# Host layouts for cached keys and up weights, and chunk weights on ScalarE's queue, in a hybrid decoder layer

## The chip, the cores and the metric

One NeuronCore of a Trainium2 chip runs the whole layer in one launch. The metric is device time in microseconds (us). All data is float32. Arrays arrive in the chip's memory in the layout that the host gives them; work of the host is outside the measured time.

## The reference, cut to what matters

The layer has 2048 prompt rows and 8 sample sequences of 4 rows each. Every sample sequence has 8192 past positions in 64 pages of 128 keys and values, found through a page table. What is computed (norms, reshapes and the prompt's own attention left out):

```python
past_k = cache_k[page_table].reshape(8, 8192, 8, 64)      # 8 heads of 64 channels
past_v = cache_v[page_table].reshape(8, 8192, 8, 64)
z = einsum('bqhd,bkhd->bhqk', q, concat(past_k, k)) * 64 ** -0.5 + sb_bias
a = exp(log_sigmoid(z) + sum of log_sigmoid(-z) over all later keys)   # stick breaking
o_sb = einsum('bhqk,bkhd->bqhd', a, concat(past_v, v))
x = x + gate1 * (concat(o_sb, o_mlp) @ w_out)              # 1024 x 1024
h2 = rms_norm(x) * (1 + scale2) + shift2
up = h2 @ w_up                                             # 1024 x 5632
g, v = split(causal depthwise convolution, width 3, of up)
y = x + gate2 * ((silu(g) * v) @ w_down)                   # 2816 x 1024
```

## The kernel before

The program has four stages, each a block in which all engines start together after the last: `prepare` (modulation vectors and constants, span 0 to about 112 us), `project_in` and `attend_prompt` (to 1263), `attend_new_keys` (the samples' own new keys, to 1286) and `finish_layer` (the rest). This change touches the first and the last two.

**finish_layer** handles the prompt in NCH = 4 chunks of CT = 512 rows, with the same plan each, and then the 32 sample rows. A chunk is: the output projection (`tok` events of phase 0: four 1 MB weight loads), the norm and its transposes (`turn`), the up projection (22 tiles f of 2 x 128 columns; a tile is seven products `mul(f, p)` of four 128x128 by 128x256 matmuls each), and the down projection (`tok` events of phase 1: 16 loads of 768 or 256 KB). A matmul of float32 shows as two records of TensorE in the trace, so a product is eight. ScalarE copies four of the seven products out of PSUM (`collect`: L1571, L1574, L1579, L1582) and applies the last tap (L1592); VectorE adds the other three (L1721, L1727, L1731) and the other taps (L1758); GpSimd makes three sums of each up tile's blocks and changes one block in place (`weight_sums`, L1814 to L1819), then multiplies the gated rows.

**Weights** go through a ring `w` of RING = 3 slots. There are LOADS = 42 loads a chunk. All are issued by SP from one list, `load_order`: load n goes where the last use of n - 3 stands in the plan, after a wait for TensorE's counter that this use is over (`wait_used`, L1331). An up tile is two DMAs of 512 KB, whose rows in memory are 128 columns, 512 bytes, long.

**The samples' past keys** are spread over the same plan. A chunk holds 16 steps (`CHUNK_STEPS`); a step takes 2 pages of 4 sequences, in all 2 MB of keys in `kpage` and 2 MB of values in `vpage`, single buffers of 8 pages. SP loads a page with a register load of its number (L954), then a DMA (L962 for keys, L964 for values). These 16 page loads of a step stand in the same list as the weights. A step is cut into pieces, put into the plan at equal distance of planned cost:

- pieces 0 to 3: VectorE turns a quarter of `kpage` into `kT` (two quarters in piece 0; L1105, 32x32 blocks), and TensorE, in pieces 1 to 4, scores it: four matmuls of 128x32 by 128x256 (L1003), one on each 32 columns of the array, which run side by side. The four quarters add up in `pZ`.
- ScalarE makes the gates (L1055, L1056) in piece 4; WEIGH (piece 5): VectorE's scan and product (L1084, L1088).
- MOVE: two TensorE transposes (L1009) and two copies by VectorE (L1095). It stands with piece 1 of the next step, behind its scores.
- SUM: eight matmuls of 128x32 by 128x512 (L1017) over `vpage`. It stands with piece 3 of the next step, behind its scores.

`kpage` is free for the next keys when VectorE has turned all four quarters (`kT_ready`), `vpage` when SUM is done (`av_done`). 100 pieces are placed in a chunk.

**The sample rows at the end** (`plan_s`) need all 42 weight loads once more, from the same ring by SP, after the store of the samples' attention and the loads of the conv state and gates. An up tile is then 8 matmuls of 128x32 by 128x256 (L1476, 16 records) and a fold (L1486).

**prepare** loads the head bias for the samples with 32 DMAs of 4 elements (L116), on SP, ahead of the loads of `x_prompt` and `w_in`, which `project_in` waits for. **attend_new_keys** rearranges queries by 16 VectorE copies (L1070) and keys by 16 ScalarE copies (L1038) into the layout of the turned pages.

Of the kernel before, what the change touches and what calls it, by code (L numbers as in the profile page):

```python
# [8 lines left out]
ACT = mybir.ActivationFunctionType  # L9
# [3 lines left out]
P = 128  # L13
D = 1024
# [35 lines left out]
def prepare(nc, sem, a, k, nxt):  # L50
# [4 lines left out]
    with ExitStack() as ctx:  # L55
# [28 lines left out]
        def _(sp):  # L84
# [43 lines left out]
            sp.wait_ge(small_loaded, 16 * (14 + 8 * TS))  # L128
# [26 lines left out]
        def _(act):  # L155
            act.wait_ge(c_loaded, 32)
            act.activation(c_sig[:], c_rows[:], ACT.Sigmoid).then_inc(c_silu, 1)
            act.wait_ge(small_loaded, 16 * (14 + 8 * TS))
# [733 lines left out]
PG = 2  # L892
# [4 lines left out]
QT = DSB // P  # L897
TURN, WEIGH, MOVE, SUM = QT - 1, QT + 1, QT + 2, QT + 3


class SampleAttention:
# [8 lines left out]
    def __init__(self, nc, sem, sb, pb, a, k, dr, out):  # L910
# [3 lines left out]
        self.q = sb("s_q", [P, 2, QT, HP, 32])  # L914
        self.kT = sb("s_kT", [P, 2, SG, PG * P])
# [4 lines left out]
        self.o = sb("s_o", [P, HP, NSEQ, TS])  # L920
        self.pZ, self.pO = [pb("s_pZ0"), pb("s_pZ1")], [pb("s_pO0"), pb("s_pO1")]
        self.k_loaded, self.v_loaded = sem("s_k_loaded"), sem("s_v_loaded")
        self.in_loaded, self.filled, self.q_ready = sem("s_in_loaded"), sem("s_filled"), sem("s_q_ready")
        self.kT_ready, self.kT_used, self.z_done = sem("s_kT_ready"), sem("s_kT_used"), sem("s_z_done")
# [6 lines left out]
    def new_inputs(self, sb):  # L931

        self.qraw, self.kraw = sb("s_qraw", [P, HP, S]), sb("s_kraw", [P, HP, S])
        self.knew = sb("s_knew", [P, 2, QT, HP, TS])
        self.vnew = sb("s_vnew", [TS, NSEQ, DSB])
# [6 lines left out]
    def sp_inputs(self, sp):  # L942
        cols = lambda t: self.dr[t][0:DSB, SEQ:SEQ + S].rearrange("(r p) q -> p r q", p=P)
        sp.dma_start(self.qraw[:], cols("qT")).then_inc(self.in_loaded, 16)
        sp.dma_start(self.kraw[:], cols("kT")).then_inc(self.in_loaded, 16)
        sp.dma_start(self.vnew[:], self.out["v_s"][0].rearrange("b s h e -> s b (h e)")).then_inc(self.in_loaded, 16)

    def sp_pages(self, sp, c, q, of_keys, j):
# [3 lines left out]
        for sl in range(SG):  # L952
            at = (SG * g + sl) * NPAGE + NPAGE - PG + j - PG * m
            page = sp.value_load(self.k["pt"][0:1, bass.ds(at, 1)], min_val=0, max_val=self.a[table].shape[1] - 1)  # L954
            src = self.a[table][0].rearrange("n p h e -> n p (h e)")[bass.ds(page, 1), :, :]
# [928 lines left out]
```

## Time and profile before

| | us |
|---|---|
| three runs | 3850.78, 3850.82, 3855.89; median 3850.82 |
| the profiled execution | 3855.71 |
| its span, first to last instruction | 3853.9 |
| TensorE (PE) busy | 3559.7, 92% of the span |
| weight load of TensorE (PEld) busy | 2064.5, 54% |
| VectorE (DVE) busy | 1731.4, 45% |
| GpSimd (POOL) busy | 1083.5, 28% |
| ScalarE (ACT) busy | 1051.3, 27% |
| DMA queues, share of 16 engines | 49.7% (SP's), 1.1% (ScalarE's) |
| mean granted clock of TensorE | 0.954 |

PEclk is the clock that TensorE was granted, as a share of 2.4 GHz (0.50 is 1.2 GHz). SPq and ACTq rows are DMA issues of these engines. Times in rows are from the start of the span.

### The profile page before, as it was taken

How to read it: one execution, taken by the hardware profiler on the slowest of the kernel's cores; microseconds unless marked ns; L12 is line 12 of the kernel's file. 1: busy time of each engine (PE TensorE's matmuls, PEld its weight loads, DVE VectorE, ACT ScalarE, POOL GpSimd, SP SyncE). 2: the span in 40 equal slices, each digit the busy share in tenths (PEclk: the TensorE clock that was granted, in tenths of full speed). 3: DMA queues.
4: the chain of work that ended last, by engine and by line, in shares of the span. 5: the costliest groups of instructions: out<-in, count | busy, mean ns of one | idle time of the engine just before them, and what ended most of it. 6: DMA issues, size and time to landing. Idle time of an engine off the chain costs nothing.

```text
span 3853.9 us, 54699 instructions
## 1 busy us (share of the span) xinstructions
PE 3559.7 (92%) x16996; PEld 2064.5 (54%) x16996; DVE 1731.4 (45%) x2719; ACT 1051.3 (27%) x2114; POOL 1083.5 (28%) x957
## 2 busy tenths in 40 slices
PE   5799999989999689999989999999999989999978
PEld 1344444456565257763357774347774437775333
DVE  1121221178788256552256652246653245663222
ACT  0222222189889022220022220012220012221011
POOL 0001010156566035540025450015541014551000
PEclk8899999999999799999999999999999999999977
DMA  7411211111100557567757657757667666666668
GB/s 286 172 47 33 68 31 33 27 65 45 46 12 2 177 143 200 158 193 207 239 144 191 184 158 215 213 175 197 173 186 213 183 208 170 189 173 188 184 202 253
DMA packets 482109, 576.43 MB, mean 150 GB/s; under 512 B 29482, under 2 KB 289778, under 8 KB 479196
## 3 DMA queue, kind: packets, MB, share of 16 engines
q1 hardware_dynamic: 477116, 555.89, 49.7%
q10 hardware_dynamic: 4704, 17.04, 1.1%
q8 instruction: 138, 2.26, 0.2%
q14 instruction: 151, 1.24, 0.1%
HBM read 538.02 MB, written 34.81 MB: 149 GB/s over the span
## 4 chain that ended last, share of the span: by engine, by line
PE 51%; DMA 5%; SPq 4%; issue 3%; DVE 3%; POOL 1%; ACT 1%; DVEq 0%; POOLq 0%; ACTq 0%
PE ff_pB L1464 24%; PE ff_pB L1415 21%; PE s_pZ L1003 3%; DMA ff_w<-in_w_up 3%; PE s_pO L1017 2%; SPq L954 2%; SPq L962 1%; DMA ff_w<-in_w_down 1%; DMA s_kpage<-in_cache_k 1%; DVE s_kT L1105 1%; SPq L964 1%; PE s_pZ L1009 0%; PE ff_pB L1429 0%; PE ff_pB L1476 0%; SPq L1331 0%
## 5 line engine op out<-in xcount | busy, mean ns | idle before, releaser
L1415 PE MATMUL ff_pB<-ff_w,ff_hidden 128*128 128x512 f32 (+1 forms) x1496 | 669.0, 599 | 9.7 <-DMA ff_w<-in_w_down 5.0
L1464 PE MATMUL ff_pB<-ff_act_in,ff_w 128*128 128x256 f32 x2112 | 516.1, 388 | 47.0 <-DMA ff_w<-in_w_up 35.6
L1814 POOL TENSOR_TENSOR ff_sums<-ff_w 128x512 f32<-128x512 f32 x88 | 116.7, 1326 | 1330.8 <-DMA ff_w<-in_w_up 1130.5
L1464 PEld LDWEIGHTS ff_pB<-ff_act_in,ff_w 128*128 128x128 f32 x2112 | 402.8, 193 | 127.9 <-issue 63.6
L1415 PEld LDWEIGHTS ff_pB<-ff_w,ff_hidden 128*128 128x128 f32 (+1 forms) x1496 | 269.8, 186 | 372.5 <-issue 357.8
L450 PE MATMUL in_pA<-in_w,in_hT 128*128 128x512 f32 (+1 forms) x1024 | 449.1, 594 | 1.0 <-DVE in_hT L569 1.0
L1105 DVE STREAM_TRANSPOSE s_kT<-s_kpage 128x1024 f32<-128x1024 f32 x256 | 309.8, 1229 | 198.2 <-DMA s_kpage<-in_cache_k 118.9
L1758 DVE SCALAR_TENSOR_TENSOR ff_conv<-ff_raw,k_vecT,ff_conv 128x512 f32<-128x512 f32 (+1 forms) x440 | 392.7, 892 | 7.8
L889 POOL TENSOR_TENSOR at_stop<-at_stop,at_left 128x512 f32<-128x512 f32 (+3 forms) x320 | 311.5, 999 | 181.5 <-ACT at_stop L829 175.6
L1464 PE MATMUL ff_pB<-ff_diff,ff_sums 128*128 128x256 f32 x1408 | 336.6, 382 | 8.5 <-DVE ff_diff L1701 5.5
L450 PEld LDWEIGHTS in_pA<-in_w,in_hT 128*128 128x128 f32 (+1 forms) x1024 | 186.4, 185 | 231.9 <-issue 230.7
L1464 PEld LDWEIGHTS ff_pB<-ff_diff,ff_sums 128*128 128x128 f32 x1408 | 263.8, 190 | 61.5 <-issue 17.1
L1415 PE MATMUL ff_pB<-ff_w,ff_act_in 128*128 128x512 f32 (+1 forms) x544 | 254.5, 621 | 30.9 <-DMA ff_w<-in_w_out 19.2
L1055 ACT ACTIVATE s_go<-s_pZ,k_bias_s 128x256 f32<-128x256 f32 (+1 forms) x66 | 30.8, 466 | 840.5 <-PE s_pZ L1003 830.7
L1826 POOL TENSOR_TENSOR ff_raw<-ff_raw,ff_conv 128x512 f32<-128x512 f32 (+1 forms) x110 | 119.0, 1081 | 492.1 <-ACT ff_raw L1617 400.8
L1592 ACT ACTIVATE ff_conv<-ff_raw,k_vecT 128x512 f32<-128x512 f32 x176 | 142.8, 813 | 358.3 <-DVE ff_raw L1731 349.7
L877 DVE TENSOR_TENSOR_SCAN at_left<-at_go,at_left,at_one 128x512 f32<-128x512 f32 x192 | 234.7, 1264 | 2.8 <-ACT at_go L829 1.0
L829 ACT ACTIVATE at_go<-at_pZ,at_bias 128x512 f32<-128x512 f32 (+3 forms) x320 | 186.0, 647 | 45.7 <-PE at_pZ L772 36.9
L1415 PEld LDWEIGHTS ff_pB<-ff_w,ff_act_in 128*128 128x128 f32 (+1 forms) x544 | 101.6, 192 | 171.5 <-issue 171.5
L829 ACT ACTIVATE at_stop<-at_pZ,at_bias 128x512 f32<-128x512 f32 (+3 forms) x320 | 187.1, 659 | 0.0
L772 PE MATMUL at_pZ<-at_kT,at_q 64*128 64x512 f32 (+3 forms) x640 | 166.8, 599 | 18.7 <-DMA at_kT<-scratch_kT 11.6
L784 PE MATMUL at_pW<-k_ident,at_stop 128*128 128x128 f32 x1088 | 164.3, 283 | 15.7 <-ACT at_wT L837 15.2
(201 smaller groups left out, 4074.1 us busy)
## 6 DMA issues: line engine op xcount, KB each, us to landing
s_kpage<-in_cache_k SPq DMA_DIRECT2D x512, 256.0 KB, 3.8
s_vpage<-in_cache_v SPq DMA_DIRECT2D x512, 256.0 KB, 3.1
ff_w<-in_w_up SPq DMA_DIRECT2D x220, 512.0 KB, 6.0
ff_w<-in_w_down SPq DMA_DIRECT2D x70, 768.0 KB, 5.0
wada<-in_w_ada SPq DMA_DIRECT2D x8, 3072.0 KB, 12.3
ff_w<-in_w_out SPq DMA_DIRECT2D x20, 1024.0 KB, 6.3
in_w<-in_w_in SPq DMA_DIRECT2D x5, 2048.0 KB, 18.6
in_x<-in_x_prompt SPq DMA_DIRECT2D x16, 512.0 KB, 5.7
```

The lines of the kernel that those rows point to most:

```text
L450: last = pe.matmul(pA[0:R, m % 2, :], hT[:, kt, t * R:(t + 1) * R], w[:, kt, col:col + DSB], start=kt == 0, stop=kt == KT - 1)
L772: last = pe.matmul(pZ[:, s % 2, e, KC - (hi - lo):KC], q[r, p, i * P:(i + 1) * P], kT[r, p, lo:hi], start=True, stop=not first_key(s))
L784: last = pe.transpose(pW[:, e, c:c + P], stop[:, s % RS, e, c:c + P], k["ident"][:])
L829: ins = act.activation(into[:, s % RS, e, c:KC], pZ[:, s % 2, e, c:KC], ACT.Sigmoid, scale=scale, bias=bias[:, sign, 2 * p + e:2 * p + e + 1])
L877: dve.tensor_tensor_scan(left[:, e, x0:x1][:, ::-1], go[:, r, e, c:KC][:, ::-1], other, first, ALU.mult, ALU.bypass).then_inc(left_ready, 1)
L889: pool.tensor_tensor(w, w, left[:, e, x0 + 1:x1 + 1], ALU.mult).then_inc(w_ready, 1)
L1105: dve.transpose(self.kT[:, part % 2, :, :].rearrange("p t (b d) -> p b t d", d=32), src).then_inc(self.kT_ready, 1)
L1415: last = pe.matmul(pB[t][0:R, :], src, w[:, n % RING, i * 512:i * 512 + 512], start=kt == 0, stop=kt == nk - 1)
L1464: last = pe.matmul(into, left[:, kt * P:(kt + 1) * P], right[:, kt, :], start=kt == 0 and p in (1, 2, 5), stop=kt == KT // 2 - 1, skip_gro ...
L1592: act.activation(conv[:, f % 2, half, :], raw[:, f % 2, half, 2:2 + CT], ACT.Identity, scale=k["vecT"][:, 196 + ft:197 + ft], bias=k["vecT ...
L1758: dve.scalar_tensor_tensor(cv, r, tap, cv, ALU.mult, ALU.add).then_inc(tapped, 1)
L1826: pool.tensor_tensor(sg, sg, conv[:, f % 2, 0, 0:W], ALU.mult).then_inc(silu_ready, 1)
```

## The change

1. **Keys.** The host lays each page of `cache_k` out with the channels in the partitions: 128 rows, each 4 head pairs x 128 keys. A page goes straight to `kpage[:, j, sl, :]` as 128 rows of 2 KB, the same bytes and row length as before. VectorE's transposes and `kT` are gone. TensorE scores from `kpage` in one piece, SCORE, with the same 16 matmuls; queries are kept per sequence instead of per quarter. A step is now four pieces (SCORE, WEIGH, MOVE, SUM), 64 in a chunk, none sharing a place. SCORE waits for all 8 pages; keys of the next step are loaded when it is done.
2. **Weights on ScalarE's queue.** In the four chunks ScalarE issues the weight loads: each where the last use of the slot stands in its own order, behind its own work there, after the same wait. The first three are issued ahead of the loads of x; the sample rows' first three come at the end of the fourth chunk. SP keeps pages, `act_in`, and the sample rows' other 39 loads.
3. **Up weights.** The host lays `w_up` out as 22 contiguous tiles of 1 MB, 8 KB for each partition: one DMA each.
4. **Small things.** 16 DMAs of 8 elements for the head bias in place of 32; 8 VectorE copies in place of 16 for the queries, and none for the new keys (24 fewer copies in all); MOVE's copy is one instruction in place of two.

```diff
@@ prepare
-            for at in range(0, 32, 2 * TS):
-                for e in range(2):
-                    for t in range(TS):
-                        row = at + TS * e + t
-                        sp.dma_start(k["bias_s"][row::32, 0:1], a["sb_bias"][0].rearrange("(h e a) -> e h a", e=2, a=1)[e],
-                                     allow_slow_non_contiguous=True).then_inc(small_loaded, 16)
+            for r in range(0, P, 32):
+                for t in range(TS):
+                    small(k["bias_s"][r + t:r + 32:TS, 0:1], a["sb_bias"][0].rearrange("(h a) -> h a", a=1))
@@ SampleAttention.sp_pages
-                    sp.wait_ge(self.kT_ready, QT * N + QT)
+                    sp.wait_ge(self.z_done, N + 2)
-                sp.dma_start(self.kpage[32 * sl:32 * sl + 32, j, :, :], src.rearrange("n (b r) e -> r (n b) e", r=32)).then_inc(self.k_loaded, 16)
+                src = self.a[table][bass.ds(page, 1), :, :].rearrange("n p e -> p (n e)")
+                sp.dma_start(self.kpage[:, j, sl, :], src).then_inc(self.k_loaded, 16)
@@ SampleAttention.pe_piece
-        if 1 <= i <= QT:
-            part = i - 1
-            if part == 0:
-                pe.wait_ge(self.wT_read, N + 1)
-            pe.wait_ge(self.kT_ready, QT * N + part + 1 + QT)
-            for tile in range(HP):
-                last = pe.matmul(self.pZ[g][32 * tile:32 * tile + 32, 0:ZC], self.q[:, g, part, tile, :], self.kT[:, part % 2, tile, :],
-                                 start=part == 0, stop=part == QT - 1)
-            last.then_inc(self.kT_used, 1)
+        if i == SCORE:
+            pe.wait_ge(self.wT_read, N + 1)
+            pe.wait_ge(self.k_loaded, 16 * UNITS * (N + 1))
+            for hp in range(HP):
+                for sl in range(SG):
+                    last = pe.matmul(self.pZ[g][32 * sl:32 * sl + 32, 0:ZC].rearrange("p (j t) -> p j t", j=PG), self.q[:, SG * g + sl, hp, :],
+                                     self.kpage[:, :, sl, hp * P:(hp + 1) * P], start=hp == 0, stop=hp == HP - 1)
+            last.then_inc(self.z_done, 1)
@@ SampleAttention.dve_piece
-        for part in {0: (0, 1), 2: (2,), TURN: (3,)}.get(i, ()):
-            if part == 0:
-                dve.wait_ge(self.k_loaded, 16 * UNITS * (N + 1))
-            dve.wait_ge(self.kT_used, QT * N + part + 1)
-            src = self.kpage[:].rearrange("p j b (t c d) -> p c (j b) t d", c=QT, d=32)[:, part]
-            dve.transpose(self.kT[:, part % 2, :, :].rearrange("p t (b d) -> p b t d", d=32), src).then_inc(self.kT_ready, 1)
@@ step_pieces
     for q in range(CHUNK_STEPS):
-        for i in range(WEIGH + 1):
-            pieces.append([(q, i)])
-            if q and i in (1, 3):
-                pieces[-1].append((q - 1, MOVE + i // 2))
-    return pieces + [[], [(CHUNK_STEPS - 1, MOVE)], [], [(CHUNK_STEPS - 1, SUM)]]
+        pieces += [[(q, SCORE)], [(q, WEIGH)], [(q, MOVE)], [(q, SUM)]]
+    return pieces
@@ new, beside load_order
+def loads_after(plan):
+    last_use = {load_of(event): at for at, event in enumerate(plan) if event[0] in ("tok", "mul")}
+    follow = {}
+    for n, at in last_use.items():
+        follow.setdefault(at, []).append((n + RING) % LOADS)
+    return follow
@@ finish_layer, load_w (now for either engine; wait_used is the same with eng for sp)
+            elif n < WO + UP:
+                dma(slot, a["w_up"][n - WO])
@@ finish_layer, SP
             order = load_order(plan_p)
+            order = [x for x in order if x[0] != "w"]
-            loads(NCH, load_order(plan_s), 1)
+            loads(NCH, [x for x in load_order(plan_s) if x[0] == "w" and x[1] >= RING], 1)
@@ finish_layer, ScalarE
             def body(c, R, nt, W, plan):
-                for kind, *which in plan:
+                follow = loads_after(plan) if R == P else {}
+                for at, (kind, *which) in enumerate(plan):
...
+                    for n in follow.get(at, ()):
+                        load_w(act, c + (n < RING), TT, n)
                 for t in range(nt):
                     store_y(c, R, nt, t)
+            for n in range(RING):
+                load_w(act, 0, TT, n)
             load_x(0, P, TT, first=True)
```

## Rows read from the trace of the kernel before

**Rows 1.** Waits of PE over the span: total us, times, longest.

```profile
PE ff_pB L1464 <- DMA ff_w<-in_w_up: 35.6, 8, 6.1
...
PE ff_pB L1476 <- DMA ff_w<-in_w_up: 15.5, 19, 3.4
...
PE s_pZ L1003 <- DVE s_kT L1105: 9.6, 5, 4.4
...
PE ff_pB L1464 <- DVE ff_raw L1721: 7.6, 8, 1.0
...
PE ff_pB L1415 <- DMA ff_w<-in_w_down: 5.0, 5, 2.0
```

**Rows 2.** Chunk 2: PE, PEld, DVE, ACT, POOL busy; PEclk; DMA share; GB/s.

```profile
1900.00:2495.00 595.00, 566.77 (x2536) 349.47 (x2536) 280.41 (x433) 107.38 (x206) 174.07 (x132) 0.98 0.66 189
```

**Rows 3.** Timeline of SP's queue ahead of a wait for up weights.

```profile
2149.41 8.98 SPq L962 DMA_DIRECT2D s_kpage<-in_cache_k  x8
2159.16 8.39 SPq L964 DMA_DIRECT2D s_vpage<-in_cache_v  x8
2167.66 5.94 SPq L1331 DMA_DIRECT2D ff_w<-in_w_up  x4
```

**Rows 4.** Timeline of PE behind that wait, in brackets the idle time.

```profile
2175.70 3.77 PE L1464 MATMUL ff_pB<-ff_act_in,ff_w 128*128 128x256 f32 x8 [5.36 <-DMA ff_w<-in_w_up]
2179.26 3.08 PE L1464 MATMUL ff_pB<-ff_diff,ff_w 128*128 128x256 f32 x8
```

**Rows 5.** Timeline of PE over a stretch of step pieces among products.

```profile
2027.98 0.44 PE L1009 MATMUL s_pZ<-k_ident,s_stop 128*128 128x128 f32 x2
2028.25 1.89 PE L1464 MATMUL ff_pB<-ff_act_in,ff_w 128*128 128x256 f32 x8
...
2031.71 1.89 PE L1464 MATMUL ff_pB<-ff_act_in,ff_w 128*128 128x256 f32 x8
2033.53 0.64 PE L1003 MATMUL s_pZ<-s_kT,s_q 128*32 128x256 f32 x8
2034.10 1.99 PE L1464 MATMUL ff_pB<-ff_diff,ff_sums 128*128 128x256 f32 x8
...
2039.48 0.64 PE L1003 MATMUL s_pZ<-s_kT,s_q 128*32 128x256 f32 x8
2039.93 1.90 PE L1017 MATMUL s_pO<-s_vpage,s_wT 128*32 128x512 f32 x16
2041.76 1.99 PE L1464 MATMUL ff_pB<-ff_act_in,ff_sums 128*128 128x256 f32 x8
```

**Rows 6.** Timeline: the head bias loads, and the query copies.

```profile
67.41 17.82 SPq L116 DMA_DIRECT2D k_bias_s<-in_sb_bias  x32
...
1269.44 2.96 DVE L1070 COPY s_q<-s_qraw 32x32 f32<-32x32 f32 x16 [3.47 <-DMA s_vnew<-out_v_s]
1273.21 0.59 PE L984 MATMUL s_pZ<-s_knew,s_q 128*32 128x4 f32 x8 [13.39 <-ACT s_knew L1038]
```

**Rows 7.** Timeline of PE at the start of finish_layer.

```profile
1302.36 9.84 PE L1415 MATMUL ff_pB<-ff_w,ff_act_in 128*128 128x512 f32 x16 [16.39 <-DMA ff_w<-in_w_out]
1316.58 1.08 PE L1003 MATMUL s_pZ<-s_kT,s_q 128*32 128x256 f32 x8 [4.38 <-DVE s_kT L1105]
```

**Rows 8.** Timeline of ACT inside one up tile, idle time in brackets.

```profile
2021.12 0.39 ACT L1574 ACTIVATE ff_raw<-ff_pB 128x256 f32<-128x256 f32 x1 [2.14 <-PE ff_pB L1464]
```

**Rows 9.** Issues of w_in's DMAs: ns least/median/most, first and last start.

```profile
L127 SPq DMA_DIRECT2D in_w<-in_w_in x5: 447/5007/5061, 93.2 to 106.2; - x5
```

**Rows 10.** Stretches as in Rows 2: w_ada's loads, sample rows' up tiles.

```profile
20.00:60.00 40.00, 21.05 (x112) 4.41 (x116) 0.00 (x0) 0.00 (x0) 0.00 (x0) 0.68 0.94 383
...
3740.00:3800.00 60.00, 49.16 (x338) 25.43 (x339) 24.43 (x136) 22.16 (x101) 8.61 (x34) 0.50 1.15 291
```

**Rows 11.** Timeline of PE in the sample rows' last up tiles.

```profile
3797.71 1.94 PE L1476 MATMUL ff_pB<-ff_w,ff_act_in 128*32 128x256 f32 x16 [0.64 <-DMA ff_w<-in_w_up]
...
3801.55 1.94 PE L1476 MATMUL ff_pB<-ff_w,ff_act_in 128*32 128x256 f32 x16 [0.91 <-DMA ff_w<-in_w_up]
```

More of the change, by code:

```diff
@@ L896 @@
 CHUNK_STEPS = 2 * MSTEPS // NCH
-QT = DSB // P
-TURN, WEIGH, MOVE, SUM = QT - 1, QT + 1, QT + 2, QT + 3
+SCORE, WEIGH, MOVE, SUM = range(4)
 class SampleAttention:
@@ L1027, in pe_end @@
             for hp in range(HP):
[L1028 removed]
+                last = pe.transpose(self.pZ[g][:, hp * P:(hp + 1) * P], self.sums[:, g, :][:, hp * P:(hp + 1) * P],
                                     self.k["ident"][:])
@@ L1236, in load_order @@
             for j in range(PG):
-                loads.append((piece_at.get((q - 1, TURN), j - LOADS), LOADS + j, ("sa", q, True, j)))
+                loads.append((piece_at.get((q - 1, SCORE), j - LOADS), LOADS + j, ("sa", q, True, j)))
                 loads.append((piece_at.get((q - 1, SUM), 0), LOADS + j, ("sa", q, False, j)))
@@ L1301, in tok, with wait_used, load_w, dma @@
             return 4 * TT * c + (2 * phase + n2) * nt + t + 1
+        def wait_used(eng, c, nt, n):
+            if n < 0:
+                c, nt, n = c - 1, TT, n + LOADS
+            if WO <= n < WO + UP and nt == 1:
+                eng.wait_ge(up_part, n - WO + 1)
+            elif WO <= n < WO + UP:
+                eng.wait_ge(up_done, NUP * c + UP_AT[n - WO, 4])
+            elif n in (1, 3, WO + UP + 7, WO + UP + 15):
+                phase, n2 = int(n >= WO + UP), int(n in (3, WO + UP + 15))
+                eng.wait_ge(tok_done, tok(c, phase, n2, nt - 1, nt) + 4 * TT)
+            else:
+                at = n // 2 + 1 if n < WO else 2 + (n - WO - UP) - (n - WO - UP) // 8 + 1
+                eng.wait_ge(w_used, 16 * c + at + 16)
+        def load_w(eng, c, nt, n):
+            wait_used(eng, c, nt, n - RING)
+            slot = w[:, n % RING, :]
+            def dma(dst, src):
+                eng.dma_start(dst, src).then_inc(w_loaded[n % RING], 16)
+            if n < WO:
+                n2, kq = n // 2, n % 2
+                src = a["w_out"][0].rearrange("(r p) n -> p r n", p=P)[:, 4 * kq:4 * kq + 4, n2 * 512:n2 * 512 + 512]
+                dma(slot.rearrange("p (r n) -> p r n", r=4), src)
+            elif n < WO + UP:
+                dma(slot, a["w_up"][n - WO])
+            else:
+                d = n - WO - UP
+                n2, f = d // 8, d % 8 * DF
+                nf = min(DF, FT - f)
+                src = a["w_down"][0].rearrange("(r p) n -> p r n", p=P)[:, f:f + nf, n2 * 512:n2 * 512 + 512]
+                dma(slot[:, 0:nf * 512].rearrange("p (r n) -> p r n", r=nf), src)
         plan_p, plan_s = chunk_plan(TT, step_pieces()), chunk_plan(1, [])
@@ L1389, in loaded @@
             def loaded(c, n):
-                per = 16 * LOADS // RING + 16 * sum(1 for q in range(WO, WO + UP) if q % RING == n % RING)
-                before = sum(2 if WO <= q < WO + UP else 1 for q in range(n % RING, n + 1, RING))
-                pe.wait_ge(w_loaded[n % RING], per * c + 16 * before)
+                pe.wait_ge(w_loaded[n % RING], 16 * (LOADS // RING) * c + 16 * (n // RING + 1))
             def project(c, R, nt, phase, n2, q, t):
@@ L1807, in weight_sums @@
                 n, at = WO + f, 4 * (FT * c + f)
-                per = 16 * LOADS // RING + 16 * sum(1 for q in range(WO, WO + UP) if q % RING == n % RING)
-                landed = sum(2 if WO <= q < WO + UP else 1 for q in range(n % RING, n + 1, RING))
                 A11, A12, A21, A22, S2, S3, S4 = weights_of(f)
-                pool.wait_ge(w_loaded[n % RING], per * c + 16 * landed)
+                pool.wait_ge(w_loaded[n % RING], 16 * (LOADS // RING) * c + 16 * (n // RING + 1))
                 if f >= 2:
```

103 lines of the change are left out of this document (31 added, 72 removed).

## The prediction, on record before the changed kernel ran

> **What bounds the kernel now.** I read the page's list of busy times first: TensorE is busy 92% of the span, no other engine over 54%. Then the busy time by stretch, to see whether that holds inside the chunks, which are some 2380 of the 3854 us: in chunk 2 TensorE is busy 566.8 of 595 us at clock 0.98, VectorE 280, GpSimd 174, ScalarE 107, the DMA engines 66% [rows 2]. So TensorE's own stream sets a chunk, plus 28 us of its waits. A VectorE instruction taken away is worth nothing by itself; a TensorE instruction shortened, or a wait of TensorE removed, is worth its whole length. Then I read TensorE's list of waits: 35.6 us in eight waits for up weights, 9.6 for turned keys, 7.6 for VectorE's add L1721, 5.0 for down weights, and in the sample rows 15.5 for up weights [rows 1]. The timelines say why the weights are late. SP issues eight key pages in 8.98 us and eight value pages in 8.39 us, from 2149.4 to 2167.6, and at 2167.66 the first up load [rows 3]; TensorE goes on at 2175.70 after 5.36 us of idling [rows 4]. The load was late in being issued.
>
> **The change, part by part.** All sums are against the profiled execution, 3855.7 us.
>
> *Head bias.* 32 issues took 17.82 us, 0.557 each [rows 6]. Sixteen fewer: 8.9 us. They stand ahead of the loads that the next stage waits for, and TensorE is idle there, so it comes off the end. The new DMA has twice the elements; if an issue cost a third more, 5.9 us would be left. **-8.9**, between -6 and -10.
>
> *New keys.* 16 query copies took 2.96 us, 0.185 each, from 1269.44; eight end at 1270.9. TensorE started at 1273.21 because it waited for ScalarE's 16 copies, which are gone [rows 6]. **-2.2**, between -1 and -3.
>
> *Start of finish_layer.* Before, TensorE made 16 records in 9.84 us, then stood for 4.38 us until keys were turned, and scored a quarter [rows 7]. SCORE now stands behind the first `tok` event, eight records, and needs all eight pages. The bytes in front of these pages are about the same (act_in 2 MB and keys 2 MB on one queue, as much of weights and x beside them), so the keys still land at about 1315. Up to then TensorE has done eight records less. They cost 8 x 0.43 = 3.4 us at full clock, double at half. **+4**, between 0 and +8.
>
> *Turning and scoring.* The product rows are 1.73 us apart when nothing stands between (3.46 for two, from 2028.25) [rows 5]. A quarter's scores alone move the next product from 1.73 to 2.39 us behind the last, and the product after them takes 0.10 longer: 0.76. From 2034.10 to 2041.76, less three products of 1.73, and 0.10 more behind it less the 0.10 that the first score left, is 2.47: scores and SUM together. Before SUM the scores last 0.45 and in front of a product 0.57; so there is 0.09 ahead, and 0.12 to 0.14 and then 0.10 behind, whenever the array goes from whole-array products to the four 32-column groups and back. MOVE behind scores is 0.27 (2027.98 to 2028.25), with no 0.10 behind: 0.93 with its scores. A step cost 0.93 + 0.76 + 2.47 + 0.76 = 4.92. A step after: SCORE 0.09 + 4 x 0.43 + 0.13 + 0.10 = 2.04, MOVE 0.29, SUM 0.09 + 1.83 + 0.10 = 2.02; together 4.35 to 4.40. I take 0.53 saved, times 64 steps: **-34**. Bounds: if MOVE and SUM standing alone each pay 0.2 more, -8; nothing in the rows gives more than -37. The transposes on VectorE are worth nothing beyond the waits that they caused, below. The keys' reads by TensorE, two runs of 128 in place of one of 256, I cost at nothing: the count of columns is the same. Keys have more time than before: the eight pages, 9 us of issue and some 4 of landing, are asked for when SCORE is done and needed four pieces (some 37 us) later.
>
> *Weights on ScalarE's queue.* The page burst of 17.5 us no longer stands ahead of them. A load is issued when product 4 of tile f is done and needed at product 1 of tile f + 3, twelve products or some 21 us later. An up load landed 6.7 us or so after issue with the half-rate rows of 512 bytes. So the eight waits go: -35.6, and I leave 1 us. Their cost is more than the idle time: after the 5.36 us wait the next two products took 3.56 and, with 0.09 for the scores behind, 3.0 in place of 1.73 each [rows 4], 3.1 us at the half clock that followed the idling. The eight waits average 4.5 us, so I give the eight some 2.3 each: -18. The 5.0 us for down weights have the same cause: -4 with their clock. What the moved step adds is 42 issues a chunk on ScalarE, in its order. Behind each stand its next copies out of PSUM, and TensorE behind those; the tight place is inside an up tile, and there ScalarE idles 2.14 us ahead of its copy L1574 [rows 8]. The lowest issue of 2 MB on SP's queue took 0.45 us and the median 5.0, when the queue was full [rows 9]. Here at most three loads are under way on the queue, so I take the low end: hidden. In the `tok` phases ScalarE now waits for TensorE at each load, and has nothing else to do. **-57**, between -35 and -62.
> The Trainium skill ("DMA: Bandwidth & Descriptors", Rules for kernel authors) says that spreading DMAs over SP, ScalarE and GpSimd does not help bandwidth, since all run on the same 16 engines, and only saves issue time. By it the transfers would still be as long; rows 3 show that issue time is what was lacking, with the engines at 66% [rows 2].
>
> *VectorE's cover.* TensorE waited 9.6 us for turned keys, 4.4 of them at the start (counted above): -5.2. It waited eight times 0.95 for the add L1721. I worked out the planner's order: twice in a chunk WEIGH stands right behind product 1 (tiles 2 and 7), which is where these waits are; in the new order once (tile 6). -3.8. **-9**, between -4 and -10. In exchange WEIGH and MOVE have a piece, some 9 us, to themselves, so no new wait.
>
> *Sample rows.* The first weights are there; what is left ahead of TensorE is the chain of stores, gates and conv state, so -1.8. In the up tiles a load of 1 MB with 512-byte rows is the limit: 291 GB/s at a DMA share of 1.15, while w_ada with its rows of 24 KB moved 383 GB/s at 0.94 [rows 10]. At 291 a tile is 3.6 us; at 383, 2.7. TensorE's own cycle is 3801.55 - 3797.71 less the wait of 0.91, 2.93 us [rows 11], at half clock, and less at full clock. 22 tiles, the first three of them loaded ahead in both: some 19 x (3.7 - 2.85) = 16. **-18**, between -2 and -23.
> The Trainium skill ("DMA: Bandwidth & Descriptors", Specifications) gives 512 bytes as the least transfer for line rate. By that rule the contiguous tiles would gain nothing here, a result of its own; it is among the rivals. Rows 10 speak against it: full engines moved 291, not 383.
>
> The sum: -8.9 - 2.2 + 4 - 34 - 57 - 9 - 18 = -125, so 3731 for an execution like the profiled one. That one stands with the upper of the two values that the runs show (3850.8 and 3855.9); from the median it is 3726. I give **3728**.
>
> **The rivals.**
> 1. *The transfers, not their issue, made the weights late.* Pages and weights now run side by side, and each up load takes a share of the engines: a load under a page burst gets half of some 290 GB/s, 7 us and more. For it: landing already takes 7 us. Against: 21 us are given. If it held, 53 of the 57 would stay: 3728 + 53 = 3781.
> 2. *Row length doesn't matter.* The mechanism: the up tiles at the end are held by memory or by the ring, not by packets of 512 bytes. The 16 us stay: 3744. Half-rate engines in rows 10 speak against it.
> 3. *The pieces pay for standing alone, or ScalarE's waits for TensorE push its gates late.* 10 to 30 us come back: 3738 to 3758.
> 4. *The other side: ScalarE's queue blocks.* If its issues last as the median of w_in's, 5.0 us [rows 9], its copies in an up tile come 5.0 - 2.14 = 2.9 us late, 88 times: +252, so 3728 + 252 = 3980. It decides from 125/88 + 2.14 = 3.6 us an issue upward. Against: w_in's were 10 MB asked for at once; here one load replaces one.
>
> **How the numbers follow.** Forecast 0.60 (its own range 3705 to 3752), rival 1 0.13, rival 2 0.10, rival 3 0.12, rival 4 0.05. The range 3697 to 3785 takes in rivals 1 to 3 and the bounds of the scoring and weight terms; what lies outside is rival 4, several terms at their low ends, and a gain above all bounds. 0.2% is 7.7 us, about what a measurement of this kernel can tell from no change. Faster by more: 0.94, within: 0.02, slower: 0.04.
>
> **What would show it.** In the profile after: the head bias issues sum to about 9 us; no transposes; SCORE blocks of 32 records in about 1.9 us, 64 of them; TensorE's wait list without up weights in the chunks; no clock below 0.9 inside them other than at the norm and the chunk's start; the DMA share below 0.66; sample up tiles some 2.8 us apart; SP's wait for SCORE long. Wrong would make it: TensorE waits for ScalarE's L1571 to L1582 with DMA issues of over 2 us on ScalarE, waits for key pages beyond the first step, or up weights still in the wait list with early issues.

## The result, and the profile after

The changed kernel takes **3696.11 us** (median of four runs, 3687.66 to 3698.75) against 3853.36 for the kernel before on the same chip (3850.78 to 3855.91): a ratio of **0.9588**, 95% interval 0.957 to 0.9607, so 157 us less. The forecast was 3728, in a range of 3697 to 3785: the direction was right, the gain 32 us larger than forecast and just beyond the range. The profiled execution is the fastest of the four (3687.66, span 3685.9). Lines have moved: L1396 is the projection (L1415 before), L1445 the up product (L1464), L1410 the turn behind the norm (L1429), L1707 VectorE's add (L1721), L997 SCORE, L1003 MOVE, L1011 SUM.

TensorE's waits after, with total us, times and the longest:

```profile
PE ff_pB L1445 <- DVE ff_raw L1707: 10.2, 16, 1.0
PE ff_pB L1457 <- DMA ff_w<-in_w_up: 7.3, 9, 1.9
PE s_pZ L997 <- DMA s_kpage<-in_cache_k: 6.8, 1, 6.8
...
PE ff_pB L1410 <- DVE ff_hidden L1672: 5.8, 7, 1.3
...
PE s_pZ L1003 <- DVE s_stop L1074: 5.1, 2, 3.8
```

No wait for up weights is left in the chunks, and none for turned keys [rows 1]. The second chunk, in the columns of [rows 2] (PE, PEld, DVE, ACT, POOL busy, PEclk, DMA share, GB/s), and the up tiles of the sample rows, to hold against [rows 10]:

```profile
1849.00:2411.00 562.00, 549.50 (x2548) 350.83 (x2544) 225.30 (x354) 105.72 (x204) 176.64 (x132) 1.00 0.61 201
...
3573.00:3633.00 60.00, 52.93 (x416) 28.14 (x416) 28.02 (x154) 27.24 (x116) 9.11 (x36) 0.60 0.90 333
```

TensorE stands still for 12.5 us of a chunk in place of 28, its own work is 17 us shorter, and the clock is 1.00. A step's three pieces, each among products that are 1.73 apart (timeline of TensorE):

```profile
1967.45 1.89 PE L1445 MATMUL ff_pB<-ff_diff,ff_sums 128*128 128x256 f32 x8
1969.27 1.93 PE L997 MATMUL s_pZ<-s_kpage,s_q 128*32 128x256 f32 x32
1971.13 1.99 PE L1445 MATMUL ff_pB<-ff_act_in,ff_sums 128*128 128x256 f32 x8
1972.96 1.89 PE L1445 MATMUL ff_pB<-ff_act_in,ff_w 128*128 128x256 f32 x8
...
1986.77 0.38 PE L1003 MATMUL s_pZ<-k_ident,s_stop 128*128 128x128 f32 x2
1986.99 1.89 PE L1445 MATMUL ff_pB<-ff_diff,ff_w 128*128 128x256 f32 x8
```

From product to product over SCORE is 1.82 + 1.86, and the product behind it takes 1.83: SCORE costs 2.05. SUM costs the same (1995.72 to 1997.58), MOVE 0.22.

Where the time went, by the starts of the first record of each stage in the two profiled executions: up to the new keys' first score 1273.2 before, 1259.4 after (-13.8); from there to the first `tok` 29.1, 25.2 (-3.9); the four chunks 2383.1, 2245.7 (**-137.4**); sample rows and end 168.4, 155.6 (-12.8). The forecast had some -11, +4, -100 and -18. Of the first, 7.0 are the head bias, 2.3 the new keys, and 4.3 stand ahead of both: SP comes to the head bias at 63.15 in place of 67.41 us, behind the loads of w_ada, which the change doesn't touch and for which TensorE waits 33.7 us before and 29.8 after (29.8 to 33.9 in the runs below). So these 4.3 us are no term of the change; the profiled executions are 168 us apart, the medians 157.

The chunks' 137 us are shorter waits and shorter work of TensorE, in about equal parts: over the four chunks it is busy for 2274.3 us before and 2202.0 after (-72), and stands still for 108.8 and 43.7 (-65).

What the forecast had no term for stands at each chunk's norm. Two lines of TensorE's list of waits before name it:

```profile
PE ff_pB L1429 <- DVE ff_hidden L1686: 19.0, 8, 2.6
...
PE ff_pB L1429 <- DVE ff_act_in L1692: 7.0, 5, 1.6
```

TensorE's timeline before, from the first transpose of the normed rows to the first up product, and ScalarE's beside it:

```profile
1969.59 0.38 PE L1429 MATMUL ff_pB<-k_ident,ff_hidden 128*128 128x128 f32 x2
1972.13 0.33 PE L1429 MATMUL ff_pB<-k_ident,ff_hidden 128*128 128x128 f32 x1 [2.15 <-DVE ff_hidden L1686]
1975.04 1.33 PE L1429 MATMUL ff_pB<-k_ident,ff_hidden 128*128 128x128 f32 x5 [2.59 <-DVE ff_hidden L1686]
1978.01 5.91 PE L1429 MATMUL ff_pB<-k_ident,ff_hidden 128*128 128x128 f32 x24 [1.64 <-DVE ff_act_in L1692]
1984.87 3.71 PE L1464 MATMUL ff_pB<-ff_act_in,ff_w 128*128 128x256 f32 x16 [0.94 <-ACT ff_act_in L1557]
```

```profile
1968.54 1.28 ACT L1055 ACT_TABLE_LOAD   x1
1969.83 0.47 ACT L1055 ACTIVATE s_go<-s_pZ,k_bias_s 128x256 f32<-128x256 f32 x1
...
1972.41 1.28 ACT L1552 ACT_TABLE_LOAD   x1
1973.71 0.29 ACT L1552 ACTIVATE ff_root<-ff_ss,k_eps 128x1 f32<-128x1 f32 x1
```

```profile
1974.90 2.37 DVE L1105 STREAM_TRANSPOSE s_kT<-s_kpage 128x1024 f32<-128x1024 f32 x2
1977.19 0.77 DVE L1692 TENSOR_SCALAR ff_act_in<-ff_pB,k_gain,k_shift 128x512 f32<-128x512 f32 x1
```

A step's gates stand between ScalarE's roots, with a table load of 1.28 us on each side, and VectorE has that step's scan and the next step's first two transposes in the middle of the norm. The stretch is 15.3 us. After:

```profile
1920.90 1.92 PE L1011 MATMUL s_pO<-s_vpage,s_wT 128*32 128x512 f32 x16
1922.75 0.44 PE L1410 MATMUL ff_pB<-k_ident,ff_hidden 128*128 128x128 f32 x2
...
1925.03 0.77 PE L1410 MATMUL ff_pB<-k_ident,ff_hidden 128*128 128x128 f32 x5 [1.31 <-DVE ff_hidden L1672]
...
1931.34 1.99 PE L1445 MATMUL ff_pB<-ff_act_in,ff_w 128*128 128x256 f32 x8 [0.87 <-ACT ff_act_in L1538]
```

It is 8.6 us. A SUM stands right in front of the first transpose here, so a part of what TensorE waited for the rows before is now filled with work: from the end of the projection to the first up product it is 15.3 us before and 10.4 after. The 26 us around it by windows (columns as above), first before, then after:

```profile
1964.00:1990.00 26.00, 17.18 (x69) 10.82 (x67) 17.51 (x25) 10.84 (x18) 0.00 (x0) 0.80 0.61 171
```

```profile
1917.00:1943.00 26.00, 22.22 (x134) 14.64 (x133) 15.22 (x20) 9.27 (x16) 4.76 (x4) 1.00 0.54 172
```

Before, three of the four norms had 10.2 us at 1.2 GHz behind them and the fourth 6.8; after, one has 3.4. Inside the chunks, without the first 5.5 us, which were at half already when they began, the granted clock was at half for 95 us before and for 20 after. TensorE was busy in 75 and 16 us of that. Half of that difference, some 29 us, is an estimate of what the clock gave.

### The profile page after: what moved, and what is told of

It reads as the page before. It is cut to its first block, busy times and chain, and to the rows that moved or that the text cites. A ratio compares the mean times of both kernels' runs of the same rounds, so it can differ in the third digit from the quotient of the medians.

```text
span 3685.9 us, 53482 instructions
## 1 busy us (share of the span) xinstructions
PE 3477.4 (94%) x16995; PEld 2067.3 (56%) x16996; DVE 1511.9 (41%) x2391; ACT 1041.0 (28%) x2090; POOL 1090.0 (30%) x957
## 4 chain that ended last, share of the span: by engine, by line
PE 59%; DMA 3%; DVE 2%; issue 1%; ACT 0%; SPq 0%; ACTq 0%; DVEq 0%
PE ff_pB L1445 29%; PE ff_pB L1396 23%; PE s_pZ L997 3%; PE s_pO L1011 3%; DMA ff_w<-in_w_up 1%; DMA out_y_p<-ff_x 1%; PE ff_pB L1457 1%; DMA s_kpage<-in_cache_k 0%; DMA ff_w<-in_w_down 0%; PE ff_pB L1410 0%; PE s_pZ L1003 0%; DVE ff_act_in L1678 0%; DVE ff_diff L1662 0%; DVE ff_conv L1744 0%; DVE ff_raw L1707 0%
## 5 line engine op out<-in xcount | busy, mean ns | idle before, releaser
L1396 PE MATMUL ff_pB<-ff_w,ff_hidden 128*128 128x512 f32 (+1 forms) x1496 | 660.4, 597 | 5.5 <-issue 2.1
L1445 PE MATMUL ff_pB<-ff_act_in,ff_w 128*128 128x256 f32 x2112 | 504.5, 382 | 13.7 <-DVE ff_raw L1707 10.2
L1396 PEld LDWEIGHTS ff_pB<-ff_w,ff_hidden 128*128 128x128 f32 (+1 forms) x1496 | 271.6, 185 | 368.7 <-issue 361.6
L1445 PEld LDWEIGHTS ff_pB<-ff_act_in,ff_w 128*128 128x128 f32 x2112 | 395.9, 190 | 91.7 <-issue 20.0
L1744 DVE SCALAR_TENSOR_TENSOR ff_conv<-ff_raw,k_vecT,ff_conv 128x512 f32<-128x512 f32 (+1 forms) x440 | 424.7, 965 | 7.7
L1445 PE MATMUL ff_pB<-ff_diff,ff_sums 128*128 128x256 f32 x1408 | 334.3, 380 | 0.0
L1445 PEld LDWEIGHTS ff_pB<-ff_diff,ff_sums 128*128 128x128 f32 x1408 | 265.6, 190 | 45.1 <-issue 10.0
L1396 PE MATMUL ff_pB<-ff_w,ff_act_in 128*128 128x512 f32 (+1 forms) x544 | 248.3, 613 | 20.2 <-DMA ff_act_in<-scratch_catT 12.5
L1070 DVE TENSOR_TENSOR_SCAN s_left<-s_go,s_left 128x256 f32<-128x256 f32 (+1 forms) x66 | 64.5, 977 | 408.5 <-ACT s_go L1043 407.1
L1396 PEld LDWEIGHTS ff_pB<-ff_w,ff_act_in 128*128 128x128 f32 (+1 forms) x544 | 101.7, 191 | 158.3 <-issue 148.9
```

Of the source, the lines that this page charges most:

```text
L1396: last = pe.matmul(pB[t][0:R, :], src, w[:, n % RING, i * 512:i * 512 + 512], start=kt == 0, stop=kt == nk - 1)
L1445: last = pe.matmul(into, left[:, kt * P:(kt + 1) * P], right[:, kt, :], start=kt == 0 and p in (1, 2, 5), stop=kt == KT // 2 - 1, skip_gro ...
L1744: dve.scalar_tensor_tensor(cv, r, tap, cv, ALU.mult, ALU.add).then_inc(tapped, 1)
```

## The experiments

In the table "chunks" is from the first `tok` of chunk 1 to the last record of chunk 4's down projection, "norm" the stretch shown above in chunk 2, both from the profiled execution. Medians are over four to six runs; the kernel before had 3854.5, 3857.7 and 3857.4 in the three groups (runs 1 to 4, 5 to 8, 9 to 12).

| run | median | ratio to before, 95% | chunks | norm |
|---|---|---|---|---|
| before | 3853.4 | 1 | 2383 | 15.3 |
| after | 3696.1 | 0.9588 (0.957 to 0.9607) | 2246 | 8.6 |
| 1 queue alone | 3827.3 | 0.9924 (0.9903 to 0.9946) | 2353 | 15.2 |
| 2 keys alone | 3717.7 | 0.9643 (0.9622 to 0.9663) | 2252 | 10.5 |
| 3 up tiles alone | 3832.4 | 0.994 (0.9921 to 0.996) | 2377 | 15.3 |
| 4 old places | 3700.6 | 0.9597 (0.9578 to 0.9616) | 2253 | 12.8 |
| 5 queue undone | 3695.9 | 0.9579 (0.9562 to 0.9596) | 2248 | 8.6 |
| 6 before, values later | 3798.2 | 0.9839 (0.9817 to 0.9861) | 2324 | 15.3 |
| 7 before, norm clear | 3838.8 | 0.9955 (0.9942 to 0.9968) | 2371 | 11.7 |
| 8 turns back | 3726.8 | 0.9661 (0.9642 to 0.9679) | 2281 | 11.5 |
| 9 SUM behind SCORE | 3669.9 | 0.9518 (0.9505 to 0.9531) | 2222 | 7.1 |
| 10 as 9, weights on SP | 3699.0 | 0.9588 (0.9575 to 0.9601) | 2246 | 7.9 |
| 11 three waits | 3671.1 | 0.9524 (0.9509 to 0.9539) | 2243 | 9.9 |
| 12 both | 3657.7 | 0.9484 (0.9471 to 0.9498) | 2223 | 7.1 |

**1. Weights on ScalarE's queue alone.**

```diff
 # kernel before, ScalarE's body
+                    for n in follow.get(at, ()):
+                        load_w(act, c + (n < RING), TT, n)   # and none of these in SP's list
```

> The kernel before with one part of the change: the chunk weights are issued on ScalarE's queue, each right behind the last use of its buffer; up weights keep their two transfers of 512-byte rows, keys are turned on the chip. As forecast (issue was late): TensorE's waits for up weights in the chunks go from 35.6 us to about 0, and with the half clock behind them and the down weights 57 to 65 us go: 3789 to 3797. If the transfers and not their issue were late (rival 1), some 4 us: about 3849. If the drop that the forecast did not account for (30 us) sat in this part: about 3765.

27 us, less than half of the 57 forecast. The waits for up weights in the chunks did go. Others grew:

```profile
PE s_pZ L1003 <- DVE s_kT L1105: 25.1, 5, 8.3
...
PE ff_pB L1477 <- DVE ff_raw L1739: 13.6, 19, 1.0
```

Turned keys were waited for 9.6 us before and 25.1 now: 8.3 at the start, then some 4.2 near the end of each chunk. The half clock inside the chunks is 85 us, not much less than 95. At the end of chunk 1 the last of a step's eight key pages is issued at 1805.4 and VectorE turns them from 1812.65, 7.3 us later; before it was 4.2 us (1818.4 and 1822.67). Transfers of both queues are under way there, so what rival 1 feared may have met the keys and not the weights; no run tests it.

**2. The keys alone.** The 32 bias transfers here fill the bias column in the kernel before's row order, so the sample rows are computed with their heads' biases exchanged; the work is the same.

```diff
 # SP's list, with weights in it, old w_up
-                loads.append((piece_at.get((q - 1, TURN), j - LOADS), LOADS + j, ("sa", q, True, j)))
+                loads.append((piece_at.get((q - 1, SCORE), j - LOADS), LOADS + j, ("sa", q, True, j)))
 # and step_pieces, sp_pages, pe_piece, dve_piece as in the change
```

> The kernel before with one part: keys laid out by channel, scored straight from the pages, in the four pieces a step of the change; weights stay on SP's queue with their old layout, and the 32 bias transfers stay. By the terms of the forecast (start +4, new keys -2, steps -34, VectorE's cover -9): -41, so 3812. If the shorter stretch at each chunk's norm (15.3 us before, 8.6 after) and the full clock behind it come with this part: another -27 and -19, so some 3765.

137 us: more than either theory. The chunks take 2252 us, against 2246 with everything changed, and up weights are waited for only in the sample rows, though SP still issues them. Its timeline says why:

```profile
2154.00 8.01 SPq L963 DMA_DIRECT2D s_vpage<-in_cache_v  x8
2162.12 1.01 SPq L1309 DMA_DIRECT2D ff_w<-in_w_up  x2
2164.09 9.85 SPq L960 DMA_DIRECT2D s_kpage<-in_cache_k  x8
```

Before, keys and values were both asked for where the last quarter is turned and SUM stands, next to each other in SP's list [rows 3]. With SUM one piece ahead of the next SCORE there is room in the list between the bursts, and a weight that falls due there goes out. The place of the pages, not the queue, looked like the cause; runs 5, 6, 9 and 10 test it.

**3. Up tiles alone.**

```diff
 # kernel before, load of an up tile, still on SP
+                dma(slot, a["w_up"][n - WO])            # 8 KB for each partition, in place of two loads of 512-byte rows
```

> The kernel before with one part: up weights as contiguous column tiles, one transfer in place of two, still on SP's queue. By the forecast -16 in the up tiles of the sample rows, and the eight waits in the chunks shorter by what a load lands sooner, about 1.2 us each, so -10: 3828. If row length did nothing: 3853, with the sample up tiles as long as before (79.7 us for 22).

22 us. The stage of the sample rows is 153.6 us in place of 168.4, so -15, as forecast from the row length. The eight waits in the chunks hardly shrink (32.2 us from 35.6): a load that lands sooner doesn't help one that is issued behind two bursts of 17.5 us in all.

**4. The old places in the changed kernel.**

```diff
     for q in range(CHUNK_STEPS):
-        pieces += [[(q, SCORE)], [(q, WEIGH)], [(q, MOVE)], [(q, SUM)]]
+        now = [[], [], [], [], [(q, SCORE)], [(q, WEIGH)]]
+        if q:
+            now[1].append((q - 1, MOVE))
+            now[3].append((q - 1, SUM))
+        pieces += now
```

> The changed kernel with SCORE, WEIGH, MOVE and SUM put at the places in the plan where the kernel before has its last quarter of scores, WEIGH, MOVE and SUM, so that in each chunk step 1's gates and WEIGH stand at the norm again; nothing else changes. If it was the places that made the norm stretch long (gates between the roots, with their table load, and WEIGH on VectorE): 8.6 us becomes 12 or more in each chunk and the half clock comes back behind it, +25 to +46, so 3720 to 3742. If it was the transposes on VectorE: within 5 us of 3696.

The norm stretch is 12.8 us in place of 8.6, with TensorE's waits for the norm's rows (L1676) at 18.9 us in eight, as before the change (those for the norm's copy, 7.0 before, stay away at 1.7), and 6.8 us of half clock behind each. But the chunks are only 7 us longer and the medians 4.5 apart, within their intervals: the old places give elsewhere what they take at the norm (MOVE's wait of 5.1 us, behind ScalarE's stores of y, is gone). So the mechanism is there and is worth less than its own theory gave it.

**5. The queue undone in the changed kernel.**

```diff
-            order = [x for x in order if x[0] != "w"]    # SP issues the weights again
```

> The changed kernel with its chunk weights back on SP's queue, among the pages in the planner's order; keys, bias and up tiles as changed. If the queue was worth what the forecast gave it (57 us, up loads late behind page bursts): up weights in TensorE's list of waits again and 3750. If, as the run of the keys alone suggests (its four chunks take 2252 us, those of the changed kernel 2246, with no wait for up weights), the keys' part takes the lateness away by itself: 3698 to 3706, no wait for up weights in the chunks.

3695.9 against 3696.1: the second theory. With the rest of the change in place the queue is worth nothing measurable.

**6. The kernel before, value pages three pieces later.**

```diff
-                loads.append((piece_at.get((q - 1, SUM), 0), LOADS + j, ("sa", q, False, j)))
+                at = piece_at.get((q - 1, SUM))
+                at = 0 if at is None else piece_at[(q + 1, 0)] if q + 1 < CHUNK_STEPS else at
+                loads.append((at, LOADS + j, ("sa", q, False, j)))
```

> The kernel before with one edit in SP's order: the value pages of a step are asked for at piece 0 of the step after next's keys' turn, three pieces (some 17 us) later than now, so that eight key pages and eight value pages no longer stand back to back. If the double burst of 17.5 us is what makes up weights late: their waits (35.6 us), those for down weights (5.0) and the half clock behind them go, so about 3795. If it is the sum of SP's issues, or something of the turned keys, the waits stay and the time with them: 3845 to 3855.

3798.2, 59 us faster, from an edit of one place in a list. No wait for up weights is left in the chunks, the one for down weights is 1.8 us, and the half clock in the chunks falls from 95 to 55 us. TensorE stands still for 41 us less and works 18 us less, of which the clock gives some 16 (busy at half for 42 us in place of 75): 59. SP's bursts stand apart:

```profile
2131.91 8.96 SPq L962 DMA_DIRECT2D s_kpage<-in_cache_k  x8
2140.98 4.69 SPq L1333 DMA_DIRECT2D ff_w<-in_w_up  x4
2146.45 9.89 SPq L964 DMA_DIRECT2D s_vpage<-in_cache_v  x8
2156.46 1.14 SPq L1333 DMA_DIRECT2D ff_w<-in_w_up  x2
```

**7. The kernel before, its norm cleared.**

```diff
 # chunk_plan: these five are taken out and put in again
+        late = [("sa", 1, 4), ("sa", 1, 5), ("sa", 2, 0), ("sa", 2, 1), ("sa", 1, 6)]
+        # (1,4) behind mul(0,1), (1,5) behind mul(0,2), (2,0) behind mul(0,6), the last two behind mul(0,5)
```

> The kernel before with five places of its plan changed in each chunk: step 1's last scores and gates, its WEIGH and step 2's first pieces stand behind the first up products in place of around the norm. If gates and WEIGH at the norm make the stretch of 15.3 us long and bring the 10.2 us of half clock behind it, each chunk becomes 8 to 11 us shorter: 3810 to 3822. If the transposes on VectorE are what loads it, at most 3 us a chunk: 3842 or more.

Between the two: 17 to 19 us by median and ratio, 12 by the chunks of the profiled execution, the slowest of the six. The stretch is 11.7 us in place of 15.3.

**8. VectorE's transposes put back into the changed kernel,** on a buffer that nobody reads.

```diff
+        if i >= 10:                                      # at the places of parts 0 to 3 before
+            dve.wait_ge(self.kT_done, 4 * N + i - 10 + 1)
+            dve.transpose(self.kT[:, 1, :, :]..., self.kT[:, 0, :, :]...).then_inc(self.kT_done, 1)
```

> The changed kernel with 256 transposes of 128x1024 put back on VectorE at the places of the kernel before, on a scratch buffer that nobody reads; SCORE and the rest stay where they are. It tells whether VectorE's 310 us of turning cost TensorE anything by themselves. If they did (waits for its copies and adds inside the up tiles and at the norm): +15 to +45, 3711 to 3740. If only the places and the wait for turned keys did: within 5 us of 3696.

+31 us by the medians, 28 by the ratios. TensorE's waits, to hold against those of the changed kernel:

```profile
PE ff_pB L1458 <- DVE ff_raw L1720: 26.9, 20, 2.1
...
PE ff_pB L1423 <- DVE ff_act_in L1691: 10.1, 6, 2.4
```

The add's wait went from 10.2 to 26.9 us, the norm's copy from 4.4 to 10.1, and the half clock in the chunks from 20 to 48 us (TensorE busy in 39 of them in place of 16, so some 11 us). That is 17 + 6 + 11 = 34, for the 35 by which the chunks grew. VectorE is busy 52% of chunk 2 here, and still a pair of transposes of 2.4 us in front of a copy that TensorE needs is felt. Together with run 4 the norm adds up: 8.6, +4.2 for the places, +2.9 for the transposes is 15.7, against 15.3 before.

The run doesn't bring back what was there before. In the kernel before, the same transposes stood beside waits for the add of 7.6 us in eight, and after the change they are 10.2, not less. So that 31 us left with the transposes is not shown by this run alone. Runs 6 and 4 bear the size out: both have the old places and no double burst, and the chunks take 2324 and 2253 us. Of these 71 us, 38 are the scoring (below), so 33 are left; TensorE's waits for turned keys fall from 9.0 to 0 and for the norm's copy from 7.8 to 1.7, those for the norm's rows stay at 18.9, and it is busy at half clock for 18 us in place of 42, some 12 us. These two also differ in the weights' queue and the up tiles, which runs 5 and 3 put at nothing and at 6 us in the chunks, so 27 to 33 us are what went with the turning.

**9 and 10. SUM right behind the next SCORE; then the same with the weights on SP.**

```diff
     for q in range(CHUNK_STEPS):
-        pieces += [[(q, SCORE)], [(q, WEIGH)], [(q, MOVE)], [(q, SUM)]]
-    return pieces
+        pieces += [[(q, SCORE)] + [(q - 1, SUM)] * (q > 0), [(q, WEIGH)], [(q, MOVE)]]
+    return pieces + [[(CHUNK_STEPS - 1, SUM)]]
```

> The changed kernel with three pieces a step in place of four: SUM of a step stands right behind SCORE of the next, without a product between, so the array goes to the 32-column groups and back once for both. Each alone took 0.09 + 1.86 + 0.10 = 2.05 us; together 3.91 if the 0.19 is the price of going there and back: 63 x 0.19 = 12 us less, 3684. Key and value pages are now asked for back to back again (some 17 us on SP); the weights are on ScalarE's queue, so by the reading of the runs before no wait for them comes of it. If it does, or if key pages then land late as with the queue alone, 3700 or more.

> The run before this one with its chunk weights on SP's queue. With four pieces a step the queue made no difference (3696 either way). If the back-to-back bursts are what makes up weights late, here it makes one: waits for up weights of 20 to 35 us come back with half clock behind them, 3715 to 3745. If the queue never matters with the keys laid out by channel: 3684, as the other.

Run 9 takes 26 us off the changed kernel, twice what was expected. From its timeline:

```profile
1993.40 1.89 PE L1445 MATMUL ff_pB<-ff_diff,ff_w 128*128 128x256 f32 x8
1995.22 1.93 PE L997 MATMUL s_pZ<-s_kpage,s_q 128*32 128x256 f32 x32
1996.97 1.90 PE L1011 MATMUL s_pO<-s_vpage,s_wT 128*32 128x512 f32 x16
1998.80 1.99 PE L1445 MATMUL ff_pB<-ff_act_in,ff_w 128*128 128x256 f32 x8
```

0.09 + 1.75 + 1.83 + 0.10 = 3.77 in place of 4.10, so a visit to the 32-column groups costs 0.33, not 0.19: SCORE itself is 1.75 when SUM follows, 1.86 when a product does. A chunk has 17 such visits in place of 32, so 60 fewer in all, 20 us; the chunks are 23 us shorter. Run 10 puts key and value pages back to back with the weights behind them on the same queue:

```profile
1757.60 9.51 SPq L957 DMA_DIRECT2D s_kpage<-in_cache_k  x8
1767.87 8.04 SPq L960 DMA_DIRECT2D s_vpage<-in_cache_v  x8
1776.03 2.79 SPq L1306 DMA_DIRECT2D ff_w<-in_w_down  x3
```

It loses 29 us to run 9, where the same edit of the queue had lost nothing in run 5, and lands between the two expectations. The late loads are not the expected ones: no up weight is waited for in the chunks, down weights are, 13.3 us in five, and 27 us of half clock are in the chunks in place of 14. Which loads fall due as a burst begins depends on the plan; that was not followed further.

**11. Three waits of the changed kernel; 12. all together.**

```diff
 # prepare: the 16 bias transfers on ScalarE, behind its first activation
+                    act.dma_start(k["bias_s"][r + t:r + 32:TS, 0:1], ...).then_inc(bias_loaded, 16)
 # SP, ahead of sa.sp_store: conv state and gates of the sample rows
+            sp.wait_ge(sa.z_done, CHUNK_STEPS * NCH + 2)
 # ScalarE, from the second chunk on, behind the gates of step 0
+                        if then_x and which == [0, SCORE]:
+                            load_x(c, P, TT)
```

> The changed kernel with three waits gone: the 16 bias transfers issued by ScalarE in place of SP (10.8 us of SP's issues ahead of the first x and w_in loads); conv state and sample gates loaded once the last SCORE is done, ahead of the store of the sample outputs (TensorE waited 13.1 us for them); from the second chunk on x loads behind the first gates of the chunk (5.1 us of waits of MOVE). If each is on the path that ends last: -5 to -10, -6 to -12 (the load of the sample rows behind the store is next), -4: 3670 to 3681. If the next thing in line is as late, 3690 or more.

> Both: SUM behind the next SCORE, and the three waits gone. If they add up: 3658 to 3670.

Run 11 is 25 us below the changed kernel by median; the profiled executions, near the highest of run 11 (3668.2 to 3679.8) and the lowest of the changed kernel, differ by 8. MOVE's wait is gone from the list (5.1 us). The 13.1 us for the sample gates are gone too, but TensorE's next row stands behind something else:

```profile
PE ff_pB L1399 <- issue: 12.0, 2, 9.9
```

The store of the sample outputs and the load of these rows behind it are as long as before. The first rows of the sample projection start 14.6 us after the last chunk in place of 19.7, and of these 5.1 us only 1.6 are left at the end of the stage (the up tiles take 62.8 us in place of 61.3). At the start, the wait for x (L548) is 11.1 us in place of 19.6. How 25 us split over the three isn't shown. Run 12 is the fastest kernel here: 3657.7, ratio 0.9484, 1% below the changed kernel; the two gains, 26 and 25 each alone, give 38 together.

## Why the prediction was wrong

*Right, and right-sized.* Head bias: 16 issues in 10.79 us, so -7.0 where 8.9 was forecast; each issue cost a fifth more, within the bound. New keys -2.3 (forecast -2.2). Scoring: a step costs 2.05 + 0.22 + 2.05 = 4.32 in place of 4.92, times 64 is -38 (forecast -34, bound -37). The start: the forecast's +4 was for keys that land when TensorE has made eight records; it waits 6.8 us there in place of 4.4, and SCORE runs at half clock behind it (3.64 us). But the first rows of the chunk come 3.9 us sooner after the new keys (12.5 us of waiting in place of the 16.4 for w_out [rows 7]). The weights' own queue has a part in it, since with it undone (run 5) this stretch is 29.1 us again; alone (run 1) it gives only 1.0, and what else it needs isn't shown. Rival 2 is out: 333 GB/s at a share of 0.90 against 291 at 1.15 [rows 10], and 15 us in run 3. By these rows the engines moved 253 GB/s for a full share with the old tiles and 370 with the new, so "half-rate" in the forecast was too strong; and run 3 makes one transfer of two besides the longer rows, so it doesn't tell the two apart. The rule of the Trainium skill ("DMA: Bandwidth & Descriptors", Specifications), by which 512-byte transfers run at line rate, doesn't fit these rows. The up tiles are 2.87 us apart in place of 3.53 (forecast 2.85); the sample rows in all gave -12.8 of -18, since the conv state and gates landed later (13.1 us of waiting in place of 9.3). Rivals 1 and 4 are out as well: up loads land 5.5 us after issue, and an issue on ScalarE takes 0.33 to 0.55 us. In rival 3, ScalarE's gates were late twice, for 5.1 us.

*Right in size, wrong in cause: the weights.* The step said: "The page burst of 17.5 us no longer stands ahead of them", and gave -57 to the queue. The lateness was worth that (run 6: -59). But the change removed it twice, by the queue and by the places of the pages, and the second alone is enough: undoing the queue costs nothing (run 5), the queue alone gives 27 (run 1), since TensorE then waits longer for turned keys (25.1 us, before 9.6) and for the add (13.6, before 7.6). The Trainium skill's rule that more queues save issue time and not bandwidth ("DMA: Bandwidth & Descriptors", Rules for kernel authors) agrees with what is left of the part: 27 us in run 1 and 29 between runs 9 and 10, where bursts stand ahead of the weights in SP's issues, and nothing where they don't.

*The step that failed:* "The transposes on VectorE are worth nothing beyond the waits that they caused", with the term "VectorE's cover" made from it, -9, out of two waits: those for turned keys (5.2) and for the add L1721 (3.8). The second came out the other way: the add's waits are 16 in place of 8, 10.2 us in place of 7.6 (VectorE's taps take 1.15 us on average in place of 1.05; why isn't shown). What was missed is the norm: I read the waits named after turned keys and left out those named after `ff_hidden` and `ff_act_in`, 19.0 and 7.0 us in the same list, behind which the same transposes and a step's gates stand. They are 5.8 and 4.4 after. With the half clock behind them, what went with the transposes is 27 to 33 us (runs 6 and 4) and what they cost when put back is 28 to 31 (run 8), in place of 9. How much of it is the transposes and how much the places is only partly shown: the norm's rows follow the places (run 4), the norm's copy the transposes (runs 4 and 8), and clearing the norm's places alone gave 12 to 19 us (run 7).

*The chunks' 137 us once more, from the waits of the two profiled executions.* TensorE stands still for 65 us less. The forecast had up and down weights (39.6 us, as forecast) and 9 for VectorE. What came there is 9.6 for turned keys, 15.8 for the norm's rows and copies, and 5.5 for `ff_diff` right behind them (L1701), less 2.6 for the add, 6.8 for the first key pages and 5.1 for MOVE; some 9 more are small waits of the projections and for ScalarE's copies. Of the 72 us less of work, 38 are scoring (forecast 34), some 29 the clock (forecast 18) and 5 have no name.

*The sum by runs:* scoring -38, double burst -59, transposes -31, sample rows -13, head bias, new keys and start -13 are -154, for -157 measured. The terms overlap and some are left out (5.2 us of waits for turned keys, which run 8 doesn't bring back; 4 to 19 us for the places at the norm), so that the sum comes this close is in part luck.

## What to carry to other kernels

Two parts of a change can remove the same stall, and each then looks worthless when it is undone: do each alone as well as undo each, and try the stall's cheapest cure by itself (here one place in a list, 59 of the 157 us). When an engine is relieved, list every wait that names any of its instructions, not only the waits for the instruction that goes; the copy that stood behind it has another name. Putting work of the same array shape side by side gave 26 us here, and lost it again when the page bursts that this lines up shared a queue with the weights (runs 9 and 10).

## What the runs showed of the hardware

Going to the 32-column groups and back costs TensorE some 0.3 us a visit (4.10 us for SCORE and SUM apart, 3.77 together). A sigmoid between square roots cost ScalarE two table loads of 1.28 us. An issue of a weight load (256 KB to 1 MB) took ScalarE 0.33 to 0.55 us, one of 8 elements took SP 0.62 to 0.74 us. At a norm TensorE idled 2.15, 2.59 and 1.64 us with little work between; its clock fell to 1.2 GHz within the second of these, at 1973.5, and stayed there for 10.2 us.
